# Reordering a layer chain: mixing sums by token tile, gating ahead of casts, modulation steps moved

## The reference

```
x = first_block(x, ...)                       # 2 x (attention, FFN)
h = x + grid_pos_emb;  mods = split(silu(c) @ w_ada + b_ada, 9)
h  = ffn_sublayer(h,  mods[0..2], g_ffn1, w_ffn1_in, w_ffn1_out)
hc = ffn_sublayer(ctx, mods_c[0..2], the same weights)
q, k, v, gates = project(h, mods[3], mods[4], w_in), and for hc
states of two directions scanned over the context, then over h
y = (sigmoid(ga) * (y_a @ w_a) + sigmoid(gb) * (y_b @ w_b)) @ w_out
h = h + mods[5] * y
h = ffn_sublayer(h, mods[6..8], g_ffn2, w_ffn2_in, w_ffn2_out)
return rmsnorm(h, g_final)
```

## Time and profile before

| | |
|---|---|
| median of 3 runs | 1699.5 us (1698.85 to 1700.06) |
| profiled execution | 1699.45 us |
| its span, first to last instruction | 1697.6 us |
| matmuls (PE) busy | 1635.0 us, 96% |
| VectorE busy | 981.7 us, 58% |
| ScalarE busy | 828.5 us, 49% |
| GpSimd busy | 149.7 us, 9% |
| HBM read | 306.77 MB, 181 GB/s over the span |
| mean granted clock | 0.987 |

### The profile page before, as it was taken

The page is one execution under the profiler, slowest core; times in us unless marked ns, Lnnn a source line. Parts: engine busy times, 40 slices in busy tenths (PEclk is TensorE's granted clock), DMA queues, the critical chain, the costliest instruction groups (busy, mean ns, idle before and its releaser), DMA issues.

```text
span 1697.6 us, 25566 instructions
## 1 busy us (share of the span) xinstructions
PE 1635.0 (96%) x10755; PEld 1461.8 (86%) x10755; DVE 981.7 (58%) x1652; ACT 828.5 (49%) x1188; POOL 149.7 (9%) x146
## 2 busy tenths in 40 slices
PE   6999999999999999999999999999999999789997
PEld 5878899987889989998799999889888888589986
DVE  4657654435645565445665666667747866455544
ACT  4556444434559745444344454444545546254442
POOL 2120001000002201110001110001000000001000
PEclk9999999999999999999999999999999999989999
DMA  8554747767663366556555667598572655645552
GB/s 274 203 199 157 260 164 245 241 211 277 210 217 115 101 235 221 179 176 216 179 174 163 200 128 205 174 182 166 126 157 67 146 170 175 229 131 184 184 164 86
DMA packets 224615, 309.46 MB, mean 182 GB/s; under 512 B 5169, under 2 KB 146854, under 8 KB 224502
## 3 DMA queue, kind: packets, MB, share of 16 engines
q1 hardware_dynamic: 221776, 300.44, 57.7%
q0 software_dynamic: 1792, 5.98, 1.2%
q10 hardware_dynamic: 934, 1.43, 0.2%
HBM read 306.77 MB, written 1.05 MB: 181 GB/s over the span
## 4 chain that ended last, share of the span: by engine, by line
PE 83%; DVE 8%; ACT 4%; DMA 2%; issue 2%; ACTq 1%; DVEq 0%; POOL 0%; POOLq 0%
PE ps L135 81%; PE ps L138 2%; DVE wl L148 2%; ACT wh L144 1%; DVE SM L158 1%; DMA raw<-in_w_in_dram 1%; ACT L144 1%; DVE MT L158 1%; DMA raw<-in_w_ffn_in_dram 1%; DVE X L158 1%; ACT SA L144 1%; ACTq L132 0%; DMA raw<-in_a_w_qkv_dram 0%; DMA raw<-in_w_ffn_out_dram 0%; DVE MT L155 0%
## 5 line engine op out<-in xcount | busy, mean ns | idle before, releaser
L148 DVE TENSOR_TENSOR wl<-raw,wh 128x1024 fp32r<-128x1024 f32 x498 | 608.1, 1260 | 446.5 <-ACT wh L144 445.8
L144 ACT ACTIVATE wh<-raw 128x1024 fp32r<-128x1024 f32 x498 | 501.1, 1052 | 255.7 <-PE ps L135 98.8
L135 PE MATMUL ps<-XTH,wh 128*128 128x256 f32 x1792 | 518.4, 289 | 4.9 <-issue 4.2
L135 PE MATMUL ps<-XTH,wl 128*128 128x256 f32 x1792 | 510.1, 285 | 0.6 <-DVE wl L148 0.6
L135 PE MATMUL ps<-XTL,wh 128*128 128x256 f32 x1792 | 510.1, 285 | 0.0
L135 PEld LDWEIGHTS ps<-XTH,wh 128*128 128x128 f32 x1792 | 346.9, 194 | 17.3 <-issue 11.4
L135 PEld LDWEIGHTS ps<-XTL,wh 128*128 128x128 f32 x1792 | 346.9, 194 | 2.5 <-issue 2.2
L135 PEld LDWEIGHTS ps<-XTH,wl 128*128 128x128 f32 x1792 | 346.8, 194 | 0.8 <-DVE wl L148 0.8
L135 PE MATMUL ps<-wh,XTH 128*128 128x512 f32 x352 | 141.4, 402 | 0.0
L135 PE MATMUL ps<-wh,HTH 128*128 128x512 f32 x352 | 139.5, 396 | 0.0
L135 PE MATMUL ps<-wl,HTH 128*128 128x512 f32 x352 | 139.0, 395 | 0.0
(11 more groups left out here) (300 smaller groups left out, 2019.5 us busy)
## 6 DMA issues: line engine op xcount, KB each, us to landing
raw<-in_w_ffn_in_dram SPq DMA_DIRECT2D x66, 1024.0 KB, 5.0
raw<-in_ffn_w_gate_up_dram SPq DMA_DIRECT2D x44, 1024.0 KB, 5.1
raw<-in_w_in_dram SPq DMA_DIRECT2D x40, 1024.0 KB, 8.4
raw<-in_w_ada_dram SPq DMA_DIRECT2D x36, 1024.0 KB, 5.0
raw<-in_w_ffn_out_dram SPq DMA_DIRECT2D x30, 1024.0 KB, 5.0
raw<-in_ffn_w_down_dram SPq DMA_DIRECT2D x20, 1024.0 KB, 5.1
raw<-in_a_w_qkv_dram SPq DMA_DIRECT2D x12, 1024.0 KB, 7.3
raw<-in_kv_w_dram SPq DMA_DIRECT2D x8, 1024.0 KB, 6.8
```

The source lines that it names most:

```text
L135: return NOTHING if self.e is None else self.e.matmul(o, l, r, start=start, stop=stop, skip_group_check=skip)
L144: return self.e.activation(o, i, fn, bias=bias, scale=scale)
L148: return NOTHING if self.e is None else self.e.tensor_tensor(o, a, b, f)
```

## The change

It has five parts.

1. `lo` takes both pieces of k 4-7 in its third step (`ends`), sums the left and right halves of token tile 0 there and those of tile 1 in the fourth step; `moving` is cut in two for it (`sums`). The evictions follow tile by tile, VectorE squares tile 0 of X between them, and ScalarE's square of tile 1 has a step of its own. `own_first` and `held` are set for the steps behind `lo`. Product 16, columns 16 and product 17 now stand ahead of the transposes of YF, in this order, and columns 17 behind the first FFN product.
2. In the first attention, modulation and context steps are LATE as well (`own_ops_first`), and the two steps that are filled come one step later.
3. Modulation steps are moved to boundaries: one behind the fill at the end of aw and of layer 0 ("gap+ada"), and one behind hq; one at aw goes. Since every fifth step of an FFN takes a modulation step and the count of 16 is reached earlier, all later ones shift; products 6 to 15 are done before the second attention's queries. Products 5 and 6 now stand around the fill after aw, 13 behind the fill of layer 0, 14 two pieces later.
4. One context step (`d8d`, left half, second part) is taken in the down sums of f1, behind the fourth piece, so the fill of the boundary behind f1 begins one step further on.
5. The four `mx_step` of the context's scan are done in the last step of the context's gates, and not ahead of its first and second token tile.

```diff
             def moving(key, wt, row, n, kts, o, XH, XL, nk, ready):
                 _, gs = piece(wsrc(wt, row + kts[0], len(kts), n, 512), len(kts), 512)
+                last = kts[-1] == nk - 1
+                order = [(i, t) for t in range(2) for i in range(len(gs))]
+                sums(key, gs, order if last else sorted(order), kts, o, XH, XL, nk, ready)
+                GROUP[key] = gs[-1]
+                look_ahead()
+
+            def sums(key, gs, order, kts, o, XH, XL, nk, ready):
                 per = len(kts) // len(gs)
                 last = kts[-1] == nk - 1
-                order = [(i, t) for t in range(2) for i in range(len(gs))]
-                for i, t in order if last else sorted(order):
+                for i, t in order:
...
-                yield from rows(n + "d", I["ffn_w_down"][layer], 0, HTH, HTL, NF, hidden_ready(n))
-                yield "gap", 2
+                for q, _ in enumerate(rows(n + "d", I["ffn_w_down"][layer], 0, HTH, HTL, NF, hidden_ready(n))):
+                    yield "ctx" if layer and q == 3 else 0
+                yield "gap" if layer else "gap+ada", 2
 
             def block2_ffn(n, w_in, w_out, first):
                 if not first:
-                    yield "last products"
+                    own_first[0] = held[0] = True
+                    yield "last", 1
+                    yield "last", 2
                 to_halves(n, blocks_of(YF), normed_ready("n" + n), shifted=True)
-                yield ("gap", 1) if first else "last sums"
+                held[0] = False
+                yield ("gap", 1) if first else None
+                own_first[0] = False
                 for q, _ in enumerate(hidden(n, w_in, XTH, XTL, half_ready(n), range(11))):
                     if q in GATE_PE:
                         gate_row("g" + n, GATE_PE.index(q))
-                    yield ("side", "conv") if first else 0
+                    yield ("side", "conv") if first else ("last", 1) if q == 0 else 0
...
-                    yield "fill" if q in (15, 16) else "ctx" if q == 14 else None if step == "t" else ("side", "d0")
+                    yield "fill" if q in (16, 17) else "ctx" if q == 14 else None if step == "t" else ("side", "d0")
...
-                    yield "ada" if q % 2 == 0 else 0
-                yield "gap", 2
+                    yield "ada" if q == 0 else 0
+                yield "gap+ada", 2
...
                 to_halves("hq", blocks_of(OA), normed_ready("n1"))
-                yield None
+                yield "ada"
...
-                for k in (0, 4):
+                for n0 in (0, 512):
+                    moving(("lo", n0), I["w_out_2"][0], 0, n0, list(range(4)), o[n0], XUH, XUL, 8, half_ready("hw"))
+                    if n0 == 0:
+                        to_halves("hw", blocks_of(GBB), lambda t, k: v_out.at("mix", t, 512), range(2, 4))
+                    yield 0
+                ends = {n0: piece(wsrc(I["w_out_2"][0], 4, 4, n0, 512), 4, 512)[1] for n0 in (0, 512)}
+                for t in range(2):
                     for n0 in (0, 512):
-                        moving(("lo", n0), I["w_out_2"][0], 0, n0, list(range(k, k + 4)), o[n0], XUH, XUL, 8,
-                               half_ready("hw"))
...
+                        sums(("lo", n0), ends[n0], [(0, t), (1, t)], list(range(4, 8)), o[n0], XUH, XUL, 8,
+                             half_ready("hw"))
+                        give(("lo", t, n0), v_out, "lo", t, n0)
+                        GROUP["lo", n0] = ends[n0][-1]
+                    look_ahead()
+                    yield 0
...
+            def own_ops_first():
+                if own_first[0]:
+                    LATE.add(len(steps))
...
-                elif want in ("last products", "last sums"):
-                    for _ in range(2):
+                elif want != 0 and want[0] == "last":
+                    for _ in range(want[1]):
+                        if own_first[0]:
+                            LATE.add(len(steps))
+                            HELD.add(len(steps))
                         next(streams["a"])
                         steps.append("a")
+                elif want != 0 and want[0] == "gap+ada":
+                    filled(want[1])
+                    ada_step()
```

On VectorE, in the same way (ScalarE and GpSimd follow):

```diff
+                if name == "cg":
+                    dve.wait_ge(*g_small.at("mst"))
+                    for d in range(2):
+                        mx_step("cu0", d, scan_tile(0, d))
+                        mx_step("cu1", d, scan_tile(1, d))
                 yield
...
                 evict = gated("lo", GB, "g5", X, MT)
-                for n0 in (0, 512):
-                    for t in range(2):
+                for t in range(2):
+                    if t == 1:
+                        squared(X, YF, S_MAIN)
+                    for n0 in (0, 512):
                         evict(t, n0)
+                    if t == 0:
+                        dve.wait_ge(*v_out.at("lo", "x", 0))
+                        dve.wait_ge(*g_out.at("lo", "x", 0))
                     yield
```

## The result

The change makes the kernel slower: 1703.73 us median of 14 runs against 1699.51 us of the kernel before on the same chip, a ratio of 1.0024 with a 95% interval of 1.0016 to 1.0032. Forecast were 1691.3 us and a range of 1685 to 1697. The profiled execution has a span of 1702.9 us where the one of before had 1697.6.

The account below looks back on a forecast made before the run. TensorE's matmuls cover 1635.0 of 1697.6 us, so only 62.6 us of idle time and the clock can change. Terms -2.8 - 1.0 - 2.6 - 1.0 - 0.5 + 0 - 3.2 + 3.0 = -8.1 us give 1691.3 us, range 1685 to 1697.

Parts of the forecast that it names:

- Last boundary: Mixing sums to second FFN of block two: split stays ahead of all four gatings, transposes come later; +3.0 us.
- Rival 1: Last boundary: casts do get out of the way, 15.6 us gained instead of 3.0 lost; 1672.7 us, chance 0.08.
- The fill moved one step: Attention A: an attention step fills the 1.92 us wait before a context product; -1.0 us, bounds -3.6 and +1.0.
- End of layer 0: Transposes at 432.19: one modulation step ahead of them fills the wait of 1.00 us; -1.0 us.
- `aw`: Transposes at 200.22: two modulation steps ahead fill waits of 1.88 and, at 209.15, 0.76 us; -2.6 us.
- attention B: Ahead of layer 1's attention: columns 15 stand in the wait of 0.88 us at 492.91; -0.5 us.
- the columns near 98: Attention A: eviction of product 2 goes before ScalarE's cast, removing columns 2's 2.89 us wait; -2.8 us, at worst 0.
- The end of layer 1: Boundary at 850.81: moving a context step into the down sums leaves the 2.21 us wait; 0, bounds -3.9 and +1.
- The context weights: Context updates near 1205: moving table load and exponentials behind the gates removes waits; -3.2 us, bounds -1.5 and -4.5.
- Rival 2: Small waits return at later late loads or casts, losing half the 11.1 us gained elsewhere; 1696.9 us, chance 0.10.
- Rival 3: `aw`, end of layer 0, `bv`: modulation loads starve the weights, 21 us if all delays are bare; 1712 us, chance 0.06.
- The strict reading: Last boundary: clock stays low for more of product 17 and the transposes, putting the term at its upper end, +4.5.

Follow-up runs that it names:

- e9: Changed kernel; at the last boundary VectorE's split and ScalarE's cast of the first FFN piece both kept until behind the norm work: 1688.52 us.
- e6: Changed kernel with the filling context product back before the last but one attention step, the count that places modulation steps kept: 1696.7 us.
- e4: Changed kernel with the modulation step at the end of layer 0 ahead of the boundary's two context products instead of behind them: 1703.83 us.
- e7: e6 without the modulation step at the end of layer 0, and with columns alone ahead of attention B: 1692.77 us.
- e8: Changed kernel with table load, exponentials and products of the context state weights back beside the value rows and updates: 1705.03 us.
- e1: Changed kernel with the filling context product back before the last but one attention step, which also shifted the count placing modulation steps: 1704.15 us.
- e10: e7 with e9's edit at the last boundary: 1679.89 us.
- e2: Changed kernel with own work first taken from modulation and context steps, main steps keeping it: 1702.05 us.

## Why the prediction was wrong

*Last boundary: right, by its own steps.* VectorE's timeline of the changed kernel has the split ahead of all four gatings, and the second gating of each token tile behind an addition of GpSimd:

```profile
1479.59 2.36 DVE L148 TENSOR_TENSOR wl<-raw,wh 128x1024 fp32r<-128x1024 f32 x2 [19.46 <-ACT wh L144]
1481.87 0.69 DVE L148 TENSOR_TENSOR MT<-ps,GB 128x512 f32<-128x512 f32 x1
1483.99 0.69 DVE L148 TENSOR_TENSOR MT<-ps,GB 128x512 f32<-128x512 f32 x1 [1.44 <-POOL X L148]
...
1489.57 0.69 DVE L148 TENSOR_TENSOR X<-X,MT 128x512 f32<-128x512 f32 x1
...
1494.11 0.75 DVE L154 TENSOR_SCALAR YF<-X,SM 128x1024 f32<-128x1024 f32 x1
```

Less the 2.0 us by which this kernel comes later to the boundary, X was forecast complete at 1487.9 and was at 1488.3, the transposes at 1494.5 and were at 1494.5. TensorE's rows behind it agree too, the product at the low clock included:

```profile
1472.83 1.92 PE L135 MATMUL ps<-raw,cT 128*32 128x512 f32 x16
1491.98 1.11 PE L138 MATMUL ps<-C,AT 128*128 128x128 f32 x4 [17.23 <-ACT AT L144]
1493.02 3.54 PE L135 MATMUL ps<-raw,cT 128*32 128x512 f32 x16
1496.49 1.97 PE L138 MATMUL ps<-C,YF 128*128 128x128 f32 x16
```

Columns 17 waited 1.18 us. The term was +3.0 and is +3.3. Rival 1 had 15.6 us to be gained on the kernel before if the splits got out of the way, 18.6 on a changed kernel that loses 3.0. The change does not do that, so its small chance was right. Its price was 3.6 us too high: e9, where the splits do get out of the way, gains 15.2 us on the changed kernel, and 12.0 on the kernel before at this place (214.7 in place of 226.8 us). Of this, 2.2 us are that the first sums start at 1482.86, 1482.2 in the time of the kernel before, and not at 1480: the cast and split of their own weights stand ahead of their shifted halves.

*The fill moved one step: the step that failed, +7.8 instead of -1.0 and far over its bound of +1.0.* I compared what the two steps wait for by the banks of the context transposes and took "some 1.3 us of waiting". The attention step also needs a value that the same engine evicts behind these transposes, and I did not look for it. e6 against the changed kernel gives 5.9 to 7.0 us for the order, 3.6 of them TensorE's idle time. That the casts of 133.67 would fall behind a Silu was seen, and its price was too small: the four casts ran at 142.97 and their second halves to 148.6, which gave the waits of 0.29 and 0.76 and, through VectorE's queue, the 2.19 in front of the transposes at 158.82.

*End of layer 0: +4.0 instead of -1.0.* "Their evictions ... which the added TensorE work covers" counted engines and not banks. A modulation step takes two of the eight PSUM banks, which `take` hands out in the order of their return. Before, four banks lay between the context sums of the left half and those of the right; with columns 12 and product 13 it is six, and the right half gets the banks of the left. VectorE frees these at 443.24, behind four second halves (timeline of VectorE of the changed kernel):

```profile
438.69 4.63 DVE L148 TENSOR_TENSOR wl<-raw,wh 128x1024 fp32r<-128x1024 f32 x4 [1.38 <-ACT wh L144]
443.24 1.28 DVE L148 TENSOR_TENSOR FT<-ps,GC 128x512 f32<-128x512 f32 x2
```

In the kernel before the same gating stood at 437.96, equally late behind its splits, and nobody waited for it. In e4, with four banks between, and in e7, without the step, the sums of the right half follow without a wait. So the failed step was to price the evictions of the added work by engine time, with nothing for the banks: a wait of 3.34 us and 1.7 of clock where I had none.

*The rest held.* `aw` -2.1 for -2.6, attention B -0.6 for -0.5, the columns near 98 -2.6 for -2.8. The end of layer 1 gained 2.0 where I had 0. It lies within its bounds and no run isolates it; 1.7 of it is a slow stretch that did not come, and the wait that I had left at 2.21 fell to 1.39. The context weights gave -3.7 in the trace for -3.2, of which e8 confirms 2.3 as waits. The other 1.7 is a slow stretch, which comes behind a wait of this length in some executions only, and not in that of e8.

*The rivals.* The result, 12.4 us over the forecast, lies between rivals 2 and 3. Rival 2, waits that come back later, has the right kind and less than half of the size (5.6 us); it named late loads, and the causes were an eviction order and banks. Rival 3, weights that come late behind modulation loads, is seen in e4 and, by a cast that waits for its load, in e1, and not at the changed kernel's two long waits. What my range lacked was a bound for a moved step that is made from its own list of needs.

On the rule of the Trainium skill (TensorE: Matmul & The Clock Gate, What's actually happening) that I weighed: product 17 ran at 3.54 us, the clock was back at 1496.3, behind 4.3 us of work, and the transposes took 1.97. The strict reading, a clock low for more of the transposes, is not borne out here.

## What to carry to other kernels

Before a step is moved into an idle stretch, write down everything that it waits for, each with the place that its producer has in its engine's order, and every shared slot (bank, buffer) that it takes, with who then gets which slot: here two fillings of 2 to 3 us each opened a wait of 3 to 5. Where a split or cast stands ahead of the work that ends a stage, look at both engines that share it; moving it on one alone leaves the other, which waits for the same load. An experiment that undoes one edit of a planner's input can shift everything that is placed by a count; compare the two plans before reading its time.

## What the runs showed of the hardware

The fall of the clock is not a function of the visible wait. A wait of 2.90 us in front of the first FFN sums was followed by full clock in e9 and by the 1.2 GHz level in e10, with the same work behind it (busy us by stretch, all engines; the number behind POOL's is the clock; e9, then e10):

```profile
1260.00:1270.00 10.00, 10.00 (x56) 8.32 (x55) 5.45 (x13) 3.77 (x4) 0.00 (x0) 1.00 0.74 126
1270.20:1273.60 3.40, 3.40 (x12) 2.85 (x11) 2.69 (x14) 2.92 (x14) 0.00 (x0) 0.50 0.97 155
1482.90:1486.30 3.40, 2.99 (x19) 2.37 (x20) 3.21 (x7) 3.36 (x6) 0.00 (x0) 1.00 1.10 348
```
```profile
1476.40:1479.70 3.30, 3.30 (x17) 3.30 (x17) 3.15 (x6) 3.26 (x6) 0.00 (x0) 0.50 1.10 347
```

The first two rows seem to show the same from the other side: 3.4 us at 0.50 behind 10 us in which TensorE counts as busy. But this busy time is not all of one kind. The timeline of TensorE of e9 has, shortly before the stretch, 16 small matmuls, of form 8*128 where most have 128*128:

```profile
1266.91 2.03 PE L135 MATMUL ps<-rT,C 8*128 8x128 f32 x16
```

All five slow stretches that begin away from any wait, between the first products and the end of the kernel (e2 at 1268.3, e4 at 1273.6, e9 at 1270.2 and 1300.9, e10 at 1264.7), begin 0.5 to 1.2 us behind the end of such a group. Most groups of this kind, two in every execution, have no slow stretch behind them. What decides between them is not shown. The longer waits leave less open: the 3.3 us in front of the context sums at the end of layer 0 came with the 1.2 GHz level in all nine traces that have them.

A stretch of 3.4 us costs 1.7 us, so one profiled execution says up to a few us more or less of a kernel than its median does; here the spans differ by 5.3 us and the medians by 4.2.
